# Output projections with y's blocks as TensorE's weights, rows as results, and x turned into columns behind layer 0

## The reference

```python
mod = silu(c) @ mod_w[layer] + mod_b[layer]
shift, scale, gate = split(mod, 3)
h = rmsnorm(x, norm_g[layer]) * (1 + scale) + shift
y = mixer(h)                       # 2048 channels, then @ w_out (2048 x 1024)
x = x + gate * y
...
return rmsnorm(x, final_g)
```

## Time and profile before

| | before |
|---|---|
| median of 3 runs | 1325.44 us |
| the profiled execution | 1325.52 us |
| its span | 1323.7 us |
| TensorE busy | 1287.9 us, 97% |
| VectorE busy | 942.8 us, 71% |
| ScalarE busy | 633.5 us, 48% |
| GpSimd busy | 308.5 us, 23% |
| TensorE in the chain that ended last | 88% |
| VectorE in that chain | 9% |
| moved by DMA | 174.15 MB |

### The profile page before, as it was taken

How to read it: one execution, slowest core, us unless ns; L and a number is a source line. 1 busy time by engine, 2 the same in 40 slices (tenths; PEclk the granted TensorE clock), 3 DMA queues, 4 the chain that set the end, 5 groups by cost and what they waited for, 6 DMA issues and landing times.

```text
span 1323.7 us, 15672 instructions
## 1 busy us (share of the span) xinstructions
PE 1287.9 (97%) x5735; PEld 1064.7 (80%) x5735; DVE 942.8 (71%) x1126; ACT 633.5 (48%) x880; POOL 308.5 (23%) x182
## 2 busy tenths in 40 slices
PE   4999999999999999999999999999999999999997
PEld 4877788888887888888888878887888888888886
DVE  6889887878878787685678796768667556335555
ACT  6465556564646464533365554244244233223654
POOL 0033443634524332030300022131232130000000
PEclk8999999999999999999899999999999999999999
DMA  9912242323232341597748212222222222853563
GB/s 308 319 48 68 64 132 64 100 84 111 68 112 76 104 132 49 196 373 231 226 158 254 72 33 64 96 64 65 96 64 64 96 64 86 312 191 111 163 223 124
DMA packets 152864, 174.15 MB, mean 132 GB/s; under 512 B 7180, under 2 KB 115924, under 8 KB 152788
## 3 DMA queue, kind: packets, MB, share of 16 engines
q1 hardware_dynamic: 152788, 173.15, 41.2%
HBM read 143.76 MB, written 29.36 MB: 131 GB/s over the span
## 4 chain that ended last, share of the span: by engine, by line
PE 88%; DVE 9%; issue 1%; ACT 1%; DMA 1%; SPq 0%; DVEq 0%; ACTq 0%
PE psum L2102 29%; PE psum L2104 28%; PE psum L2103 28%; DVE X L1458 1%; PE psum L2228 1%; DVE w_lo L1368 1%; PE psum L2420 1%; DMA whole_x<-in_x 1%; DVE X L1464 1%; DVE w_lo L1391 0%; DVE w_lo L1383 0%; DVE macc L1483 0%; DVE win L1935 0%; DVE d_lo L1953 0%; DVE bufs L1602 0%
## 5 line engine op out<-in xcount | busy, mean ns | idle before, releaser
L2102 PE MATMUL psum<-X,w_hi 128*128 128x512 f32 x1396 | 547.4, 392 | 7.7 <-DVE bufs L1420 2.2
L2103 PE MATMUL psum<-X,w_hi 128*128 128x512 f32 x1396 | 544.1, 390 | 0.0
L2104 PE MATMUL psum<-X,w_lo 128*128 128x512 f32 x1396 | 544.1, 390 | 0.0
L2102 PEld LDWEIGHTS psum<-X,w_hi 128*128 128x128 f32 x1396 | 262.6, 188 | 66.3 <-issue 8.8
L2104 PEld LDWEIGHTS psum<-X,w_lo 128*128 128x128 f32 x1396 | 262.5, 188 | 55.0
L2103 PEld LDWEIGHTS psum<-X,w_hi 128*128 128x128 f32 x1396 | 262.6, 188 | 54.4 <-issue 0.5
L1368 DVE TENSOR_TENSOR w_lo<-raw,w_hi 128x1024 fp32r<-128x1024 f32 (+2 forms) x98 | 104.9, 1072 | 136.2 <-ACT w_hi L857 135.9
L857 ACT ACTIVATE w_hi<-raw 128x1024 fp32r<-128x1024 f32 (+2 forms) x98 | 89.7, 916 | 189.0 <-PE psum L2104 170.7
L880 ACT ACTIVATE w_hi<-ssum 128x512 fp32r<-128x512 f32 x140 | 87.1, 626 | 113.6 <-PE psum L2104 81.2
L1391 DVE TENSOR_TENSOR w_lo<-ssum,w_hi 128x512 fp32r<-128x512 f32 x140 | 117.2, 843 | 24.5 <-ACT w_hi L880 23.8
L814 POOL TENSOR_TENSOR ssum<-ssum,raw 128x512 f32<-128x512 f32 x35 | 55.7, 1591 | 329.3 <-DVE w_lo L1391 329.3
(11 more groups left out here) (240 smaller groups left out, 1831.8 us busy)
## 6 DMA issues: line engine op xcount, KB each, us to landing
raw<-in_hy_w_in SPq DMA_DIRECT2D x48, 512.0 KB, 5.1
raw<-in_pool_w_in SPq DMA_DIRECT2D x32, 512.0 KB, 5.2
bufs<-y_dram SPq DMA_DIRECT2D x48, 256.0 KB, 4.1
whole_x<-y_dram SPq DMA_DIRECT2D x48, 256.0 KB, 3.4
aux<-in_mod_w SPq DMA_DIRECT2D x16, 512.0 KB, 3.9
y_dram<-bufs SPq DMA_DIRECT2D x16, 512.0 KB, 2.7
raw<-in_hy_w_out SPq DMA_DIRECT2D x16, 512.0 KB, 5.0
raw<-in_mod_w SPq DMA_DIRECT2D x16, 512.0 KB, 5.4
```

Of the source, the lines that this page charges most:

```text
L2102: nc.tensor.matmul(out_, whi, xhi, start=first, stop=False, skip_group_check=check)
L2103: nc.tensor.matmul(out_, whi, xlo, start=False, stop=False, skip_group_check=check)
L2104: return nc.tensor.matmul(out_, wlo, xhi, start=False, stop=last, skip_group_check=check)
```

## The change

**Products.** Both output projections have the roles turned: y's block of 128 positions is the stationary operand and the weight rows (512 output channels) are the moving one. The result is a block of 128 positions by 512 channels, x's own layout in memory. A pass takes whole blocks of positions: layer 0 three passes with 3, 3 and 2 blocks (18, 18 and 12 matmuls a step), layer 1 two passes with 4 each (24 a step). Each pass loads and splits all 1024 columns of a weight step. The last 2 steps of a pass (3 in the last one) are done block by block, so that blocks end one after another.

**Residual.** It is made in rows: bank x gate, with the gate as a row that is equal on all partitions, then plus x, loaded as rows from the input (layer 0) or from `x_dram` (layer 1). Squares and their sum are one ScalarE instruction for each block. Spill, reload and GpSimd's multiplication of the normalized x are gone, and so are the std product, the row sums and the broadcasts. Layer 0's gate and layer 1's gate are each summed and spread by two products of ones with 512 columns (`row_sums`); layer 1's is written to memory (`gate_dram`) and read back on all partitions. The other modulation sums have 16 columns, behind step 5 of pass B.

**Turning.** The normalized rows of layer 0's result are transposed into columns (`turn`), 3 blocks behind each of 8 steps of pass B, 3 behind each of 8 steps of pass C, and the last 2 between V1, G0 and the second halves of V0 and V1. ScalarE's `modulate` reads them from PSUM. At the end nothing is transposed: each block of rows is squared, scaled (`row_out`) and stored.

The core of the diff:

```diff
+BLOCKS = {(0, "A"): (0, 1, 2), (0, "B"): (3, 4, 5), (0, "C"): (6, 7), (1, "A"): (0, 1, 2, 3), (1, "B"): (4, 5, 6, 7)}
+LAST = {(0, "A"): 2, (0, "B"): 2, (0, "C"): 2, (1, "A"): 2, (1, "B"): 3}
+MODS_AT = {**{n: (n - 3,) for n in range(3, 13)}, **{16 + n: (10 + n,) for n in range(6)}}
...
+            def residual(layer, b):
+                for half, cols in enumerate(HALVES):
+                    at = o_count(layer, b, half)
...
+                    dve.wait_ge(*full(("O", layer, b, half)))
+                    nc.vector.tensor_tensor(XN[layer][b][:, cols], area(("O", layer, b, half)),
+                                            (gate1 if layer else gate0)[:, cols], ALU.mult).then_inc(part_made, 1)
+                    dve.wait_ge(part_made, at)
+                    dve.wait_ge(xr_in[b % 4], 16 * (2 * layer + b // 4 + 1))
+                    nc.vector.tensor_tensor(XR[layer][b][:, cols], XR[layer][b][:, cols], XN[layer][b][:, cols],
+                                            ALU.add).then_inc(o_evac, 1)
...
+            def row_out(b):
+                inverse(1, b)
+                dve.wait_ge(rstd_ready, SB + b + 1)
+                nc.vector.scalar_tensor_tensor(out=XN[1][b], in0=XR[1][b], scalar=rstd[:, 2, b:b + 1], in1=final,
+                                               op0=ALU.mult, op1=ALU.mult).then_inc(row_ready, 1)
...
             passes(0, 3)
             split_lo(("V0", 0))
             split_lo(("V1", 0))
-            for m in PASS_OUTS["C"]:
-                residual(0, "C", m, 1)
-            add_squares(0, 1, PASS_OUTS["C"])
+            low_h1(1, KB - 1)
+            gate_of_layer_1()
+            residual(0, 6)
+            inverse(0, 6)
+            residual(0, 7)
+            inverse(0, 7)
             split_lo(("G0", 0))
...
+            for b in range(4, SB):
+                residual(1, b)
+                row_out(b)
...
+                ins = products(area(name), Y_HI[layer][at % YS][:, rows], Y_LO[layer][at % YS][:, rows],
+                               w_hi[:, es + half, :], w_lo[:, es + half, :], n == 0, n == 2 * KB - 1)
...
+            def row_sums(name):
+                for half, cols in enumerate(HALVES):
+                    ins = nc.tensor.matmul(psum[:, BANKS[name][half], :], ones[:, :], acc0[:, cols], start=True, stop=True)
+                ins.then_inc(psum_full, 1)
...
                 v0, v1, g0 = ("V0", 0), ("V1", 0), ("G0", 0)
-                pe.wait_ge(o_evac, o_count(0, "B", 4))
+                pe.wait_ge(gate1_ready, 1)
                 pe.wait_ge(lo_done, HI[v0])
-                pe.wait_ge(h_ready, 2 * KB)
-                whole(v0, 0, range(5))
-                sum_rows(0, 1)
-                whole(v0, 0, range(5, KB))
-                pe.wait_ge(o_evac, o_count(0, "C", 7))
+                pe.wait_ge(h_ready, 3 * KB)
+                whole(v0, 0)
+                pe.wait_ge(o_evac, o_count(0, 6, 1))
+                pe.wait_ge(hx_ready, 3 * KB)
                 pe.wait_ge(lo_done, HI[v1])
-                whole(v1, 0, range(1))
-                broadcast(1)
-                whole(v1, 0, range(1, KB))
+                whole(v1, 0)
+                for k in range(4):
+                    turn(2, k)
+                pe.wait_ge(o_evac, o_count(0, 7, 1))
                 pe.wait_ge(lo_done, HI[g0])
                 whole(g0, 0)
+                for k in range(4, KB):
+                    turn(2, k)
```

More of the change, by code:

```diff
@@ L155, in build @@
         add_pair(q)
-    STEPS = [(layer, p, k) for layer in range(2) for p in PASSES
+    STEPS = [(layer, p, k) for layer, p in BLOCKS
              for k in ((TIME_ORDER if layer == 0 else GROUP_ORDER) if p == "A" else range(2 * KB))]
@@ L477, in full, with o_count @@
         def full(name):
-            if name[0] == "O" and name[3] == PASS_OUTS[name[2]][-1]:
-                last = [s for s in STEPS if s[:2] == name[1:3]][-1]
+            if name[0] == "O" and name not in FULL:
+                last = next(s for s in reversed(STEPS) if s[0] == name[1] and name[2] in BLOCKS[s[:2]])
                 return o_step, Y[last] + 1
             return psum_full, FULL[name]
-        def o_count(layer, p, n):
-            return 2 * KB * layer + (KB if p != "A" else 0) + n + 1
+        def o_count(layer, b, half):
+            return 2 * SB * layer + 2 * b + half + 1
         def w_used(unit):
@@ L636, in y_load @@
                 layer, p, k = step
-                first = Y[step] % (6 * KB) == 0
+                first = p == "A" and k == 0
                 at = Y[step] % YR
@@ L1170, in squares @@
-            def squares(layer, half, blocks):
-                for n in blocks:
-                    square(layer, half, n)
-                if layer:
-                    for n in blocks:
-                        scale_g(half, n)
-            def root(layer, half):
-                act.wait_ge(*full(("sum", layer, half)))
-                nc.scalar.activation(sd[:, layer + 1, 4 * half:4 * half + 4], area(("sum", layer, half))[:, 0:4],
-                                     ACT.Sqrt, scale=1.0 / D, bias=cst[:, 0:1]).then_inc(root_done, 1)
@@ L1349, in _ @@
             passes(1, 2)
-            squares(1, 1, (5, 6, 7))
-            root(1, 1)
-            row_out(4)
-            row_out(7)
+            for b in range(4, SB):
+                squares(1, b)
         @block.vector
@@ L1876, in passes @@
[L1876 to L1886 removed]
+                        if p == "B" and at in (2, 3, 4):
+                            inverse(0, at - 2)
@@ L2088, in _ @@
             passes(1, 2)
-            for m in PASS_OUTS["C"]:
-                residual(1, "C", m, 1)
-            add_squares(1, 1, PASS_OUTS["C"])
-            inverse(1, 1)
-            for b in (5, 6):
-                dve.wait_ge(*full(("row", b)))
-                nc.vector.tensor_scalar(ob[b], area(("row", b)), rstd[:, 2, b:b + 1], None, ALU.mult)\
-                  .then_inc(row_dve, 1)
+            for b in range(4, SB):
+                residual(1, b)
+                row_out(b)
         @block.tensor
@@ L2216, in sum_rows @@
-            def sum_rows(layer, half):
-                name = ("sum", layer, half)
-                pe.wait_ge(o_evac, o_count(*{(0, 0): (0, "A", 6), (0, 1): (0, "B", 1), (1, 0): (1, "A", 5),
-                                             (1, 1): (1, "B", 4)}[layer, half]))
-                pe.wait_ge(ssq_added, KB * (2 * layer + half + 1))
-                for b in range(4):
-                    ins = nc.tensor.matmul(area(name)[:, b:b + 1], SSQ[layer][:, b * P:(b + 1) * P], ones[:, 0:1],
-                                           start=b == 0, stop=True, skip_group_check=True)
+                                 (mixed_done, GB * GROUPS))[2 * b + half])
+                else:
+                    pe.wait_ge(o_evac, o_count(1, b - 4, half))
```

701 lines of the change are left out of this document (343 added, 358 removed), and 3 rows, old and new, of the table BANKS.

## The result

The changed kernel takes **1338.21 us** (median of 4 runs, 1334.92 to 1339.64), the kernel before 1325.95 in the runs beside it: ratio 1.0088, 95% interval 1.0068 to 1.0108, so 12 us slower. Forecast were 1331.4 and 1325 to 1338. The direction was right, the size was half of what came, and the range was missed by 0.2 us.

The account below looks back on a forecast made before the run. TensorE, busy 97% of the span, was taken to bound the kernel through its work, waits and tail. Terms of -6.8 - 0.7 + 3.7 + 0.5 + 2.4 + 3.0 + 1.0 + 0.5 + 2.3 = +5.9 gave 1331.4 us, range 1325 to 1338.

Parts of the forecast that it names:

- Small TensorE work: Whole kernel: broadcasts, row sums, old transposes and sums gone (22.8 us), new sums, gates and transposes 16.0: -6.8 us.
- Handover: Start of pass A of layer 0: TensorE waits 2.6 us at step 2 and 1.1 at step 4, +3.7 us.
- DMA: Pass A of layer 0: loads at the edge of the queues' rate, cost 0 to 2 us, taken as +0.5.
- Residual joints: Layer 0: VectorE's longer residuals delay splits, waits of 0.6 us in pass B and 1.8 in pass C, +2.4.
- Behind layer 0: Before layer 1's first products: wait for layer 1's gate, +3.0 us, then for G0's split behind residuals and roots, +1.0.
- Tail: End of kernel: four output chains of 5.95 us do not fit 4.1 us block spacing; 15.3 us against 13.0, +2.3.
- the signs that were to show the forecast: New profile: waits of 2 to 3 us at y and V0, outputs 6 us apart, modulation sums in 4.5 us or less.
- The third one: Rival: waits lower TensorE's clock, each such fall costing 2.3 us; two falls give 1336 us; chance 0.15.
- the second: Rival: joints partly hidden (waits 5 to 8 us), modulation sums keep full clock; 1324 to 1327; chance 0.20 together with rival 4.
- Rivals 1 and 4: 1: joints cost nothing, 1320.8 us, chance 0.08. 4: output chains overlap better, 1325.8, chance 0.20 shared with the second.

Follow-up runs that it names:

- tiles at 128: Changed kernel with the unused last small tile taken out, so the large tiles begin at a multiple of 128 bytes: 1329.03 us.
- tiles at 64: Changed kernel with the last small tile 32 bytes larger, so the large tiles begin at a multiple of 64 bytes: 1334.89 us.
- tail reordered: Against tiles at 64: at the end VectorE takes the residual of block b+1 ahead of the output of block b; 1332.30 us.
- y alone +32 and +64: Against tiles at 128: only y's pieces used as weights in layer 0 begin 32 or 64 bytes later; 1334.98 and 1333.66 us.

## Why the prediction was right or wrong

**The step that failed** is the sentence "Shape and number of the large matmuls stay (768 for each output projection, 512 columns each), so what counts is small products, waits and the tail". Shape and number did stay; the price did not, because the change moved operands by 32 bytes. 768 + 384 products at 0.0067 and 96 at 0.0030 are 8.0 us, two thirds of the 12.3 and more than the 6.8 by which the forecast missed. The experiments show it from both sides: +8.4 for the kernel before, and for the changed one 3.4 above the kernel before where it had been 12.3. (Of the 9.7 between the spans of those two profiles, 1.6 are clock; the pitches give 7.3, as y came back to 0.2276 and not to 0.2267.) It is also 8 us in which the idea of the change has no part: with the tiles at 128 the change costs 3.4 us (0.29%, 0.17 to 0.40), and 1331.4 would have been 2.4 too high, inside the forecast's own bounds.

That it would have come so near is in part luck. In the profiled executions waits, DMA and tail came out about 6.6 us cheaper than priced, and the clock (1.1 at the sums, 1.7 behind V0) and the start (3.5, of which the change's part is not shown) took back about 6.3.

Point by point:
- *Small TensorE work, -6.8.* The row sums, broadcasts and transposes are as priced; layer 1's projection came out at -4.9 against -5.0. The modulation sums cost 6.7, not 5.6, in the profiled run.
- *Handover, +3.7.* 2.3 and 0.5: right in place, 0.9 too high. The slow pitch is not the reason: with the tiles at 128 the two waits are 2.4 and 0.4.
- *DMA, +0.5.* No wait of TensorE on a transfer stands in the passes.
- *Residual joints, +2.4.* Only 0.5 in the changed kernel (pass C), and 1.1 with the tiles at 128, presumably as TensorE is faster there and wants VectorE's results sooner. I had the waits at twice their size.
- *Behind layer 0, +3.0 and +1.0.* 2.8 for the gate; G0's 1.0 did not appear, but did at once (1.2) when the gate's wait and the slow clock were taken away.
- *Tail, +2.3.* The four chains came (5.68 each, 5.95 forecast), the end did not: four chains 0.27 shorter are 1.1, and I carried a store of 4.2 over where 3.1 were to come. Interleaving them is worth 4.8.

Of the signs that were to show the forecast, the waits came (2.3 and 2.8), and so did the outputs some 6 us apart with the last one 10.3 us behind the last matmul; the modulation sums took 4.60 us, just over the 4.5.

**Rivals.** The third one, that waits lower TensorE's clock, came true in part and belonged into the forecast. Behind the wait of 2.8 the 48 products of V0 and V1 took 12.3 to 12.4 us in five profiles (the changed kernel, tiles at 64, tail reordered, y alone +32 and +64) and 10.8 in one (tiles at 128); in the five without the wait they took 10.7. Of the second, one half came: the joints' waits sum to 6.5 us (2.3, 0.5, 0.5, 2.8, and 0.4 in layer 1), within its 5 to 8 and not the 10.6 of the forecast; the other half did not, since the sums lost the clock. Rivals 1 and 4 did not occur. No rival had an operand's address in it.

The forecast that would have been right from what was open to view: the two small tiles stood in the diff, and the sizes of the tiles ahead can be added up. What was not open to view is the price, as the operands of the 512-column products in the trace of before all lay at multiples of 128.

## What to carry to other kernels

When a change alters a small tile, look where the large ones behind it now begin, and where you can, keep TensorE's operands at multiples of 128 bytes: here 32 bytes cost 8 us, more than all the new waits together. When busy time rises though work was taken away, read the pitch of the commonest instruction in each stage before any wait, and look first at instructions that the change did not touch. A queue of residual, root, output per block is best written with the next block's residual ahead of this block's output (4.8 us here), and one-column products in short groups between full ones (8 at a time kept the clock here, 16 mostly did not).

## What the runs showed of the hardware

- The pitch of a 128x512 fp32r matmul with its own weight load is 0.2267 us when both operands begin at multiples of 128 bytes. With the weights 32 or 64 bytes past one it is 0.2333 (y alone moved). With weights at 128 and columns 32 past it is 0.2333, with columns 64 past 0.2290 (the kernel before, y and d). With both operands past (xc and g) it is 0.2297 at 32 and 0.2304 at 64: no more than with one.
- The Trainium skill (SBUF — State Buffer, Operand start alignment) asks that an operand begin at a multiple of its element size, and adds "This is about legality, not speed". All kernels here keep that rule; the speed differs by 3% between places that it treats alike. Why a place off a multiple of 128 costs time is not settled by these runs.
- How often the half clock followed, over the profiles of the changed kernel's variants: behind the wait of 2.8 us ahead of V0 in five of six; behind the wait of 2.3 to 2.4 at step 2 in five of nine (18 products in 5.4 to 5.6 us, else 4.0); behind one of 1.3 there in none of two. Behind the wait of 2.1 at 135 to 137 us it followed in ten of fourteen, behind one of 2.1 at step 4 not (one profile). Behind a group of 16 one-column products (3.5 to 4.6 us) in seven of eight, behind groups of 8 (1.7 us) in none of three profiles. It fits that the changed kernel's four runs spread over 4.7 us and the old one's four over 1.4 (15 runs over 2.2), but as one execution of each kernel has a profile, that this makes the spread is not shown.
